# Modulation units in turns of two and one in the gated slots, behind the additions in the down slots, and eight in place of four in the stick-breaking projections

## The reference

```python
def ada_modulation(c, ada_w, ada_b):                 # ada_w is 1024 x 6144, one per layer
    m = jax.nn.silu(c) @ ada_w + ada_b
    return jnp.split(m, N_MOD, axis=-1)              # shift, scale, gate for mix and for ffn

def even_layer(x, c, ...):                           # odd_layer: stick-breaking attention in place of the mix
    sh_m, sc_m, g_m, sh_f, sc_f, g_f = ada_modulation(c, ada_w, ada_b)
    h = modulate(rms_norm(x, mix_norm), sh_m, sc_m)
    ...
    x = x + g_m[:, None, :] * y
    hf = modulate(rms_norm(x, ffn_norm), sh_f, sc_f)
    return x + g_f[:, None, :] * ((jax.nn.silu(hf @ w_gate) * (hf @ w_up)) @ w_down)
```

## Time and profile before

| | us |
|---|---|
| median of three runs | 1188.12 (1185.74 to 1188.53) |
| the profiled execution, whole | 1177.91 |
| its span, first to last instruction | 1176.3 |
| TensorE busy in the span | 1161.4 (99%) |
| VectorE busy | 882.2 (75%) |
| ScalarE busy | 633.7 (54%) |
| GpSimd busy | 98.4 (8%) |

### The profile page before, as it was taken

How to read it: one execution, slowest core, us unless ns; L and a number is a source line. 1 busy time by engine, 2 the same in 40 slices (tenths; PEclk the granted TensorE clock), 3 DMA queues, 4 the chain that set the end, 5 groups by cost and what they waited for, 6 DMA issues and landing times.

```text
span 1176.3 us, 22917 instructions
## 1 busy us (share of the span) xinstructions
PE 1161.4 (99%) x9553; PEld 1124.4 (96%) x9553; DVE 882.2 (75%) x1177; ACT 633.7 (54%) x853; POOL 98.4 (8%) x147
## 2 busy tenths in 40 slices
PE   8999999999999999999999999999999999999998
PEld 8999999999998999999999999999988779999998
DVE  5876778878766778778889887887777657866543
ACT  6657566633447576633558554343556665543432
POOL 0000001110034001011100001111000000000000
PEclk9999999999999999999999999999999999999999
DMA  8452568887662577787653658868846505576362
GB/s 312 156 179 72 180 220 281 303 309 247 233 233 73 180 252 256 278 317 282 234 181 129 192 159 298 277 233 297 274 147 246 181 5 188 184 262 212 120 198 84
DMA packets 150060, 248.96 MB, mean 212 GB/s; under 512 B 5554, under 2 KB 80923, under 8 KB 149979
## 3 DMA queue, kind: packets, MB, share of 16 engines
q1 hardware_dynamic: 135858, 197.17, 49.8%
q0 software_dynamic: 13952, 50.60, 11.7%
q10 hardware_dynamic: 168, 0.04, 0.0%
HBM read 246.74 MB, written 1.05 MB: 211 GB/s over the span
## 4 chain that ended last, share of the span: by engine, by line
PE 85%; DVE 5%; issue 1%; ACT 1%; DMA 1%; POOL 0%; DVEq 0%; POOLq 0%
PE ps L2153 25%; PE ps L2155 25%; PE ps L2154 25%; DVE w_lo L1262 3%; PE ps L2439 2%; DVE scratch L1764 1%; PE ps L2305 1%; PE ps L2755 1%; ACT w_hi L747 1%; PE ps L2421 1%; DMA ada_raw<-in_l_ada_w 1%; PE ps L2729 1%; PE ps L2408 1%; PE ps L2771 1%; PE ps L2238 0%
## 5 line engine op out<-in xcount | busy, mean ns | idle before, releaser
L1262 DVE TENSOR_TENSOR w_lo<-raw,w_hi 128x2048 fp32r<-128x2048 f32 (+4 forms) x196 | 412.9, 2145 | 94.3 <-ACT w_hi L747 94.0
L747 ACT ACTIVATE w_hi<-raw 128x2048 fp32r<-128x2048 f32 (+4 forms) x196 | 342.1, 1791 | 159.4 <-PE ps L2155 148.8
L2153 PE MATMUL ps<-h_both,w_hi 128*128 128x256 f32 (+1 forms) x1296 | 361.6, 279 | 2.8 <-DVE w_lo L1262 2.1
L2155 PE MATMUL ps<-h_both,w_lo 128*128 128x256 f32 (+1 forms) x1296 | 359.7, 278 | 0.0
L2154 PE MATMUL ps<-h_both,w_hi 128*128 128x256 f32 (+1 forms) x1296 | 359.7, 278 | 0.0
L2153 PEld LDWEIGHTS ps<-h_both,w_hi 128*128 128x128 f32 (+1 forms) x1296 | 242.8, 187 | 4.2 <-issue 3.4
L2155 PEld LDWEIGHTS ps<-h_both,w_lo 128*128 128x128 f32 (+1 forms) x1296 | 244.0, 188 | 0.0
L2154 PEld LDWEIGHTS ps<-h_both,w_hi 128*128 128x128 f32 (+1 forms) x1296 | 242.9, 187 | 0.1
L2153 PE MATMUL ps<-a_both,w_hi 128*128 128x256 f32 x864 | 239.1, 277 | 0.0
L2155 PE MATMUL ps<-a_both,w_lo 128*128 128x256 f32 x864 | 238.6, 276 | 0.0
L2154 PE MATMUL ps<-a_both,w_hi 128*128 128x256 f32 x864 | 238.6, 276 | 0.0
(11 more groups left out here) (425 smaller groups left out, 1814.6 us busy)
## 6 DMA issues: line engine op xcount, KB each, us to landing
ada_raw<-in_l_ada_w POOLq DMA_DIRECT2D x96, 512.0 KB, 7.0
raw<-in_mlp_w_up SPq DMA_DIRECT2D x32, 1024.0 KB, 6.6
raw<-in_mlp_w_down SPq DMA_DIRECT2D x32, 1024.0 KB, 6.4
raw<-in_l_ffn_w_gate SPq DMA_DIRECT2D x22, 1024.0 KB, 5.5
raw<-in_l_ffn_w_up SPq DMA_DIRECT2D x22, 1024.0 KB, 9.2
raw<-in_l_ffn_w_down SPq DMA_DIRECT2D x16, 768.0 KB, 5.7
raw<-in_l_w_qkv SPq DMA_DIRECT2D x12, 1024.0 KB, 6.7
raw<-in_l_w_in SPq DMA_DIRECT2D x10, 1024.0 KB, 6.3
```

The lines of the kernel that those rows point to most:

```text
L747: nc.scalar.activation(w_hi[:, s.slot, cut], raw[:, s.slot, cut], ACT.Copy).then_inc(split_hi, 1)
L1262: nc.vector.tensor_tensor(w_lo[:, s.slot, cut], raw[:, s.slot, cut], w_hi[:, s.slot, cut].bitcast(F32), ALU.subtract).then_inc(split_lo, 1)
L2153: nc.tensor.matmul(to, sh, mh, start=first, stop=False, skip_group_check=True)
L2155: return nc.tensor.matmul(to, sl, mh, start=False, stop=last, skip_group_check=True)
```

## The change

The same 96 units run in the same order, at other places of VectorE's program. In the gated slots of the first layer hidden(j) runs two units for even j and one for odd j (14 in place of 18); in the second layer one for each j up to 9 as before. In the down slots of the first layer the two units of a turn stand at its end, behind the second split (and behind the modulation of turn 0), and not at its start. In the projections one unit stands between the two reductions of slots 1, 2 and 3, and the last turn (j = 4) runs two units (8 in place of 4).

```diff
                     if j < 10 or l == 0:
-                        ada_units(2 - l)
+                        ada_units(2 if l == 0 and j % 2 == 0 else 1)
                     dve.wait_ge(parts_done, s.before + 2)
...
                 for i in range(3):
-                    if l == 0:
-                        ada_units(2)
                     split(Slot(f"ffn_down{l}", 2 * i + 2))
                     add(i)
                     split(Slot(f"ffn_down{l}", 2 * i + 3))
                     if l == 0 and i == 0:
                         modulation(2)
+                    if l == 0:
+                        ada_units(2)
                 if l == 0:
...
                         ins = nc.vector.tensor_reduce(sb_ms[:, 0, b, :], sb_sq[:, b, :].rearrange("p (h d) -> p h d", h=8),
                                                       AX.X, ALU.add)
+                        if b == 0 and j >= 1:
+                            ada_units(1)
                     link(ins)
...
                 if 1 <= j < 5:
-                    ada_units(1)
+                    ada_units(1 + (j == 4))
```

## The result

The changed kernel took 1176.08 us (median of 22 runs, 1170.02 to 1186.91) and the kernel before 1183.81 (22 runs, among them the three of the prediction; 21 lie from 1172.95 to 1188.78, one took 1867.88). The lowest runs stand 2.9 us apart. The profiled execution took 1172.61 us, 5.3 less than that of before (1177.91).

A forecast was written before the change was run, and what follows sets the result against it. VectorE was taken to bound the first layer's gated slots by 0.7 us a pair, TensorE being 99% busy overall. Terms -2.8 + 0.1 = -2.7 us, off the 1188.12 us median, gave 1185.4 us, range 1180.0 to 1189.0.

The forecast's parts named there:

- The three waits: First layer's gated slots: TensorE's later three waits on w_lo vanish, with their slower restarts; minus 2.8 us.
- The tail: Last down turn: units and fold now precede the norm's sum, using up VectorE's reserve; plus 0.1 us, at most 0.5.
- Down slot 4: Down slots: its split, now behind two units and a fold, still comes in time; nothing, 0.4 us in the range.
- Projections and stick-breaking: Added units fit VectorE's waits and the first soft sums stay in time with 0.4 us reserve; nothing.
- Rival (c): Projections: a unit waits for its late load and delays the stick-breaking; 3.4 us cost, 1188.8 us; chance 0.07.
- Rival (b): Down-slot tail and stick-breaking start take back about half, leaving 1.0 to 1.5 us gained, 1186.9 us; chance 0.15.
- Rival (a): TensorE's own work is the wall and its waits return elsewhere; nothing gained, 1188.1 us; chance 0.12.

The follow-up runs named there:

- a2: Kernel before with only the gated-slot turns of two and one and the extra projection units, down slots in old order; 1171.95 us, ratio 0.9948.
- a4: The changed kernel again with no edit, for a second profile; 1172.31 us, ratio 0.9981 to the kernel before.
- c4: Same kernel as a2, run again with more rounds; 1180.98 us, ratio 0.9967 to the kernel before.
- a3: Kernel before with only the down-slot units moved behind the additions and second split; 1176.55 us, ratio 0.9995.
- c2: The kernel before again with no edit, for a third profile; 1182.45 us, ratio 1.0006.
- d2: The kernel before again with no edit, on another chip; 1176.99 us, ratio 1.0004.
- c1: The changed kernel again with no edit, more rounds; 1182.38 us, ratio 0.9978 to the kernel before.
- d1: The changed kernel again with no edit, on another chip; 1171.78 us, ratio 0.9969 to the kernel before.
- a1: The kernel before again with no edit, for a second profile; 1178.18 us, ratio 1.0004.
- b2: Changed kernel plus two dummy VectorE multiply-adds in every first-layer gated slot from 2 to 10; 1189.69 us, single execution.
- b3: Changed kernel plus two dummy VectorE multiply-adds behind the last down-slot units, ahead of the norm's sum; 1183.93 us, single execution.
- b4: Changed kernel plus two dummy VectorE multiply-adds behind the last projection units, ahead of the capping; 1170.92 us, single execution.
- b1: Changed kernel plus two dummy VectorE multiply-adds in first-layer gated slots 3, 5, 7 and 9; 1173.1 us, ratio 0.9973 to the kernel before.
- c3: Changed kernel plus eight groups of four tiny matmuls into an unused bank where runs of slots begin; 1176.3 us, ratio 0.9974 to the kernel before.
- d3: Changed kernel plus the same eight groups of tiny matmuls as c3, on another chip; 1173.99 us, ratio 0.9977 to the kernel before.

## Why the prediction came out as it did

**The three waits, -2.8 us: right.** They are gone in the traces of after, a2, a4 and c4, and there in the traces of before, a3, c2 and d2. (c1 and d1 have none either, but they are at the long pitch, where a1 lost its later two as well.) The stretch is 3.0 us shorter where both kernels run at the short pitch (157.20, 157.14 against 154.23, 154.14, 154.21, 154.21). I had 2.7 with the tail. The split after slot 3 ends at 722.0 (722.2 predicted), and b2 brings the waits back with the load.

**The tail, +0.1: right in size, and its reserve was mis-sized.** 850.31 against 853.27 is 2.96 us, the shift of everything ahead of it. b3 shows 0.4 to 0.5 us more of reserve than the zero that I took.

**Down slot 4, nothing: right, for a wrong reason.** ScalarE's wait of 7.20 us for the load of down slot 3 is gone in after, and I had put that down to the unit loads moving behind it. But in three further traces of the unchanged kernel it isn't there either; a1's timeline of ScalarE:

```profile
809.17 2.65 ACT L747 ACTIVATE w_hi<-raw 128x1408 fp32r<-128x1408 f32 x2 [5.12 <-PE ps L2155]
```

c2 and d2 read the same (TensorE as the releaser, 5.12 and 4.87 us), and so does a2 with the old order of the down units. The late load was that one execution's. A term was argued on a row that one profile had by chance; it cost nothing here, because the term was zero either way.

**Projections and stick-breaking, nothing: right.** The second reduction of slot 3 comes 0.6 us later relative to TensorE (48.01 us behind the first product of the projections in a4, 47.37 in before; 0.8 predicted); the first sum starts without a wait, and b4 puts the reserve at 0.2 to 0.3 us (0.4 predicted). Rival (c) did not occur: the units' loads in the projections landed after 6.1 to 8.0 us in after and 8.1 at most in any trace, under the 8.5 that it needed. The estimate of 3.2 us from the Trainium skill (DMA: Bandwidth & Descriptors, Anatomy of one DMA) is half of what these traces show, with weight loads in flight beside them. Rival (b) did not occur either: no reserve ran out. Rival (a) is refuted: a2 is faster with an interval wholly below 1, and the stretch is 3.0 us shorter. The Trainium skill (Perfetto Trace Analysis, Identifying the Most-Contended Engine) says to improve the engine of highest occupancy, here TensorE. I had read this as nothing to gain while its matmuls stay; the runs refute that reading, not the rule. The gain came from ending TensorE's waits, by relieving the engine at 75% where it was the local bound.

**The step that failed** is the last one of the sum: "None of the terms depends on what lies between these two, so I take the same 2.7 us off the median". What lay between the profiled 1177.91 and the median 1188.12 was not indifferent.

First, the level. Three runs are no median of a kernel whose executions spread from 1171 to 1194 us; in the other batches the same kernel had medians of 1183.81, 1175.88, 1174.79, 1181.96 and 1175.75 us. The forecast is 1185.4 - 1176.08 = 9.3 us too high. Of this 1188.12 - 1183.81 = 4.3 us is the base alone; the other 5.0 are a difference of the two medians of 7.7 us (5.9 by the ratio) where I had 2.7. My range went 5.4 us below the forecast, with the level of three runs as its middle.

Second, the sum had no term for TensorE's own pitch, and the gain depends on it (3.0 us or, by the estimate, next to none). Pitch also makes most of the spread that the median is taken of. Reckoned from the starts, with 0.0045 us for each product of 128x256 in a long run and 0.0043 for each of 128x512, the long runs cost 1.9 to 12.1 us in the five traces with the old gated turns (before, a1, a3, c2, d2) and 1.6 to 14.1 in the six with the new ones (after, a2, a4, c1, c4, d1). The spans are 1171.3 to 1180.6 and 1168.4 to 1179.9 us; less this cost they are 1167.9 to 1170.0, mean 1169.2, and 1165.6 to 1167.2, mean 1166.4. So the change is worth 2.8 us by this estimate, and the two groups no longer overlap.

What this leaves open is a gain by the pitch itself: if a restart behind a wait can begin a long stretch, a kernel without these waits is spared some of them. For it: in the first modulated layer, from the start of gated slot 4 to that of down slot 0, over all 17 traces, TensorE restarted 17 times behind a late w_lo from the short pitch, and 5 of the 17 went on at the long one (one each in a1, a3, c2, b1 and b2). Of the slot boundaries with no gap 84 came from the short pitch and 30 from the long one, and at none of them did it change. c2's restart costs it 3.1 us against before. Of the traces that enter the stretch at the short pitch the five with the waits have a mean of 158.24 us and the four without 154.20: 4.0 us, of which 1.0 are the long runs of a1, a3 and c2. Against a large effect: over all six without waits the mean is 155.51, so that the difference is 2.7 us, no more than the waits themselves, since c1 and d1 came into the stretch at the long pitch already. And a change of pitch needs no wait: at the start of gated slot 3, six of the eight traces that came to it long and without a gap went short there. In the second layer, whose code is the same, two traces of five with the waits (before, a1) have a long run of 100 us or more and none of the six without; but b3, which has no such waits, has one too, as has b2 with them. So the 2.3 us of the profiled pair are chance as far as these runs can tell.

What the change is worth, then: the four measurements of after are 0.995, 0.9981, 0.9978 and 0.9969. Weighted by their intervals they make 0.9966 +- 0.0015, **4.0 us, 2.2 to 5.8**. The 3.0 us that the waits explain lie inside; the first measurement's 5.9 was at the high end of what such a kernel gives. The lowest runs of each batch say the same: 2.9, 2.5, 1.4 and 2.7 us apart. **Open** is whether the 1 us between 3.0 and 4.0 is anything, and what sets the pitch.

## What to carry to other kernels

Where the averages say that nothing can be won, work out both engines' time for one period of a stretch: 0.7 us of a 22.6 us pair is invisible at 99% busy, and moving work of the second engine to where it has slack takes it back. Before a sum of a few us is put on a median, ask what the executions of that kernel differ in; a row found in one profile (a late load, a wait's size) is worth a second profile before a term rests on it. Where a bound can itself run at two speeds, price the change at each.

## What the runs showed of the hardware

The products of 128x256 run one after another at 0.1133 or 0.1178 us, with the same instructions, no idle time and a granted clock of 1.00; products of 128x512 (the first slot of the projections in d2 and in after) at 0.229 or 0.233 us, the same 0.004 us more for each matmul. A pitch lasts from a few us to some 200 (a2 is long from 381 to 584 us). From gated slot 4 to down slot 0 of the first modulated layer it changed only behind a gap (a late w_lo, or c3's and d3's groups) and at none of the 114 boundaries without one; at the start of slot 3 it changed in six traces with no gap. The 0.0045 us make 0.4 us a slot and, by the estimate above, 1.6 to 14.1 us of a kernel. The 16 added groups of tiny matmuls in c3 and d3 were all followed by the short pitch, but only two of them were reached at the long one; of the six traces that reached the kernel's own group ahead of down slot 2 at the long pitch, five went short behind it and c2 stayed long. What lies behind the pitch isn't shown.

The first product behind a wait is followed after 0.22 us by the second, where the others follow after 0.11. In c3 the first product behind the tiny group has the same, 713.86 to 714.08, with no wait at all.
